# Gather of the sample tile with both parts in one set of rows, and router and low-rank weights as 32 columns

## The reference, cut to what matters

```
# GLA: forget gate through rank 16
gk = log_sigmoid(lr @ w_gk2 + b_gk2) / 16          # lr = x @ w_in[:, 3072:3088]
# MoE: the router picks one group of four experts, then two experts in it
scores = sigmoid(x @ router_w)                     # 16 experts
y = sum_e combine[:, e] * (silu(x @ w_gate[e]) * (x @ w_up[e])) @ w_down[e]
```

## Time and profile before

| | |
|---|---|
| median of 3 runs | 1433.52 us (1432.91 to 1434.7) |
| the profiled execution, its own time | 1435.86 us |
| its span | 1434.1 us |
| PE busy | 1362.3 us, 95%, 7747 instructions |
| PE weight loads | 1138.9 us, 79% |
| DVE busy | 1025.6 us, 72% |
| ACT busy | 763.7 us, 53% |
| POOL busy | 120.1 us, 8% |
| granted TensorE clock, mean | 0.992 |

### The profile page before, as it was taken

One profiled execution on the slowest core, in us unless ns is written; L12 is line 12 of the kernel. 1 busy time (PEld: TensorE's weight loads), 2 busy tenths in 40 slices (PEclk: granted clock), 3 DMA queues, 4 the chain that ended last, 5 costly groups with the idle time before them and its releaser, 6 DMA issues.

```text
span 1434.1 us, 19792 instructions
## 1 busy us (share of the span) xinstructions
PE 1362.3 (95%) x7747; PEld 1138.9 (79%) x7747; DVE 1025.6 (72%) x1097; ACT 763.7 (53%) x788; POOL 120.1 (8%) x194
## 2 busy tenths in 40 slices
PE   6999999999889999999999999999889999999996
PEld 5879898779767788888887799778767788888884
DVE  4444766773547889888898365783548889898986
ACT  4343642432433677676777363332434677676775
POOL 6000045400000000000000014200000000000000
PEclk9999999999999999999999999999999999999998
DMA  8774454425884499899894346435883699898981
GB/s 262 248 233 151 145 177 144 133 91 176 315 331 177 169 335 348 330 337 331 333 343 171 117 151 206 129 118 176 347 323 124 230 336 343 326 348 324 337 335 37
DMA packets 99699, 343.72 MB, mean 240 GB/s; under 512 B 5984, under 2 KB 32112, under 8 KB 70432
## 3 DMA queue, kind: packets, MB, share of 16 engines
q1 hardware_dynamic: 96416, 331.90, 64.5%
q0 software_dynamic: 3200, 10.68, 2.3%
HBM read 327.61 MB, written 14.94 MB: 239 GB/s over the span
## 4 chain that ended last, share of the span: by engine, by line
PE 82%; DVE 11%; ACT 4%; issue 2%; DMA 1%; SPq 0%; DVEq 0%; ACTq 0%
PE ps L1733 64%; PE ps L2211 2%; PE ps L2066 2%; PE ps L2253 1%; PE ps L2088 1%; PE ps L2123 1%; PE ps L1742 1%; DVE mix_s L1460 1%; PE ps L2076 1%; PE ps L2153 1%; DVE x L1198 1%; PE ps L1741 1%; DVE x L1195 1%; PE ps L2202 1%; PE ps L1816 1%
## 5 line engine op out<-in xcount | busy, mean ns | idle before, releaser
L1733 PE MATMUL ps<-w_hi,xt_hi 128*128 128x512 f32 x704 | 280.1, 398 | 14.4 <-DVE w_lo L1131 7.8
L1733 PE MATMUL ps<-w_hi,xt_lo 128*128 128x512 f32 x704 | 276.1, 392 | 0.0
L1131 DVE TENSOR_TENSOR w_lo<-raw,w_hi 128x2048 fp32r<-128x2048 f32 x65 | 148.6, 2294 | 149.1 <-ACT w_hi L740 149.1
L1733 PE MATMUL ps<-w_lo,xt_hi 128*128 128x512 f32 x640 | 251.1, 392 | 0.0
L740 ACT ACTIVATE w_hi<-raw 128x2048 fp32r<-128x2048 f32 x65 | 123.8, 1913 | 163.7 <-PE ps L1733 92.8
L1135 DVE TENSOR_TENSOR moe_lo<-moe_in_raw,w_hi 128x2048 fp32r<-128x2048 f32 x72 | 164.3, 2291 | 29.5 <-ACT w_hi L747 29.3
L1135 DVE TENSOR_TENSOR w_lo<-raw,w_hi 128x2048 fp32r<-128x2048 f32 x72 | 164.9, 2292 | 25.3 <-ACT w_hi L747 24.0
L1733 PEld LDWEIGHTS ps<-w_hi,xt_hi 128*128 128x128 f32 x704 | 133.3, 189 | 45.6 <-issue 10.6
L747 ACT ACTIVATE w_hi<-moe_in_raw 128x2048 fp32r<-128x2048 f32 x72 | 138.1, 1918 | 51.0 <-PE ps L1733 51.0
L1733 PEld LDWEIGHTS ps<-w_hi,xt_lo 128*128 128x128 f32 x704 | 133.2, 189 | 28.6
L747 ACT ACTIVATE w_hi<-raw 128x2048 fp32r<-128x2048 f32 x72 | 137.5, 1912 | 12.0 <-PE ps L1733 12.0
(11 more groups left out here) (380 smaller groups left out, 2375.6 us busy)
## 6 DMA issues: line engine op xcount, KB each, us to landing
raw<-in_moe_w_gate SPq DMA_DIRECT2D x48, 1024.0 KB, 4.9
moe_in_raw<-in_moe_w_down SPq DMA_DIRECT2D x48, 1024.0 KB, 4.9
moe_in_raw<-in_moe_w_up SPq DMA_DIRECT2D x32, 1024.0 KB, 4.9
raw<-in_moe_w_up SPq DMA_DIRECT2D x32, 1024.0 KB, 4.9
raw<-in_xattn_w_kv SPq DMA_DIRECT2D x16, 1024.0 KB, 5.3
raw<-in_hgrn_w_in SPq DMA_DIRECT2D x16, 1024.0 KB, 5.7
raw<-in_cache_mem_k SPq DMA_DIRECT2D x16, 1024.0 KB, 4.9
moe_in_raw<-in_moe_w_gate SPq DMA_DIRECT2D x16, 1024.0 KB, 4.9
```

The costliest lines, as they stand in the source:

```text
L1131: nc.vector.tensor_tensor(lo_at(slot_of(k)), raw_at(slot_of(k)), hi_at(hi_slot(k)).bitcast(F32), ALU.subtract).then_inc(w_low, 1)
L1733: ins = mm(out, lhs, rhs, start=start and n == 0, stop=stop and n == 2, skip_group_check=shared)
```

## The change

1. **Gather.** The sample tile's low part no longer goes to `xn_lo` but to the rows 64 to 127 of `xn_hi`'s third tile, which were zeros. DVE copies the slot numbers of its 64 tokens to these rows too, so one product with `pick` adds both parts. Each gather has five products in place of six. `comb4` gets zeros in these rows, so that "cw" doesn't count a token twice.
2. **Router and low-rank weights.** High and low parts stand side by side as 32 columns, and `both` issues two products for each k-tile in place of three: 32 columns with the high activations, 16 columns (the high ones) with the low activations. The result has 32 rows whose halves have to be added. For the gate this is done by holding `w_gk` twice, in 32 rows (one more small DMA); for the router by multiplying with `pair_sum`, two unit matrices on top of each other, in fp32, where there was a transpose.

```diff
-        w_gk = sb("w_gk", [16, 512])
-        lr_hi = sb("lr_hi", [P, KT, 16], F32R)
-        ...
+        w_gk = sb("w_gk", [32, 512])
+        pair_sum = sb("pair_sum", [2 * EXPERTS, EXPERTS])
+        lr_both = sb("lr_both", [P, KT, 32], F32R)
+        r_both = sb("r_both", [P, KT, 2 * EXPERTS], F32R)
+        lr_hi, lr_lo = lr_both[:, :, 0:16], lr_both[:, :, 16:32]
+        r_hi, r_lo = r_both[:, :, 0:EXPERTS], r_both[:, :, EXPERTS:2 * EXPERTS]
# POOL, at the start
-                     (w_gk[:, :], a["gla_w_gk2"][0]),
+                     (w_gk[0:16, :], a["gla_w_gk2"][0]),
+                     (w_gk[16:32, :], a["gla_w_gk2"][0]),
+            link(nc.gpsimd.memset(pair_sum[:], 0.0))
+            select(pair_sum[:], 1.0, 0, [[-1, EXPERTS]], 1, ALU.not_equal)
+            select(pair_sum[:], 1.0, -EXPERTS, [[-1, EXPERTS]], 1, ALU.not_equal)
# ACT
-                    nc.scalar.activation(st_moe["xn_hi"][:, t, :], x[:, t, :], ...
+                    nc.scalar.activation(st_moe["xn_hi"][0:live(t), t, :], x[0:live(t), t, :], ...
-                nc.scalar.activation(m["rt"][:], ps[0:EXPERTS, 4, 0:TILES * P], ACT.Copy).then_inc(rt_c, 1)
+                nc.scalar.activation(m["rt"][:], ps[0:2 * EXPERTS, 4, 0:TILES * P], ACT.Copy).then_inc(rt_c, 1)
# DVE
-                    nc.vector.tensor_tensor(m["xn_lo"][:, t, :], x[:, t, :], m["xn_hi"][:, t, :].bitcast(F32), ...
+                    low = m["xn_lo"][:, t, :] if t < 2 else m["xn_hi"][64:P, t, :]
+                    nc.vector.tensor_tensor(low, x[0:live(t), t, :], m["xn_hi"][0:live(t), t, :].bitcast(F32), ...
+                link(V_.tensor_copy(u_slot[64:P, 2:3], u_slot[0:64, 2:3]))
-                ins.then_inc(rt_comb, 1)
+                link(ins)
+                V_.memset(comb4[64:P, 2, :], 0.0).then_inc(rt_comb, 1)
# PE
+            def both(out, w, n, hi_x, lo_x, kt):
+                for m_, (rows, v) in enumerate(((2 * n, hi_x), (n, lo_x)) if kt < KT - 1 else ((n, lo_x), (2 * n, hi_x))):
+                    ins = mm(out[0:rows], w[:, 0:rows], v, start=kt == 0 and m_ == 0, stop=kt == KT - 1 and m_ == 1, skip_group_check=True)
+                return ins
# keep_busy
-                pe.wait_ge(rt_w, 1)
-                rows = r_hi[:].rearrange("p k e -> p (k e)")
+                pe.wait_ge(rt_w, 2)
+                rows = r_both[:, 0:4, :].rearrange("p k e -> p (k e)")
# low rank, router
-                        ins = three(ps[0:16, 7, 0:NT], lr_hi[:, kt, :], lr_lo[:, kt, :], xt_hi[:, kt, 0:NT], xt_lo[:, kt, 0:NT], kt == 0, kt == KT - 1, True)
+                        ins = both(ps[0:32, 7, 0:NT], lr_both[:, kt, :], 16, xt_hi[:, kt, 0:NT], xt_lo[:, kt, 0:NT], kt)
-                    ins = three(ps[0:EXPERTS, 4, 0:TILES * P], r_hi[:, kt, :], r_lo[:, kt, :], ...
+                    ins = both(ps[0:2 * EXPERTS, 4, 0:TILES * P], r_both[:, kt, :], EXPERTS, xt_hi[:, kt, :], xt_lo[:, kt, :], kt)
-                    ins = nc.tensor.transpose(ps[:, 5, t * EXPERTS:(t + 1) * EXPERTS], m["rt"][:, t * P:(t + 1) * P], ident[0:EXPERTS, 0:EXPERTS])
+                    ins = mm(ps[:, 5, t * EXPERTS:(t + 1) * EXPERTS], m["rt"][:, t * P:(t + 1) * P], pair_sum[:], start=True, stop=True)
# gather
-                            for r, xx in enumerate((m["xn_hi"], m["xn_lo"])):
+                            for r, xx in enumerate((m["xn_hi"], m["xn_lo"])[0:2 - t // 2]):
```

More of the change, by code:

```diff
@@ L248, in decoder_step @@
         b_gk = sb("b_gk", [P, 4])
-        w_gk = sb("w_gk", [16, 512])
-        lr_hi = sb("lr_hi", [P, KT, 16], F32R)
-        lr_lo = sb("lr_lo", [P, KT, 16], F32R)
-        r_hi = sb("r_hi", [P, KT, EXPERTS], F32R)
-        r_lo = sb("r_lo", [P, KT, EXPERTS], F32R)
+        w_gk = sb("w_gk", [32, 512])
[4 more added lines that the diff above has]
+        r_hi, r_lo = r_both[:, :, 0:EXPERTS], r_both[:, :, EXPERTS:2 * EXPERTS]
         r_bias = sb("r_bias", [P, EXPERTS])
@@ L295, in decoder_step @@
             if l == 1:
-                m["lr_t"] = m["rn"][0:16, :]
+                m["lr_t"] = m["rn"][0:32, :]
             m["states"] = [m["s0"][:, b] for b in range(2 + l)]
@@ L308, in decoder_step @@
             "xn_hi": ([P, TILES, D], F32R), "xn_lo": ([P, TILES, D], F32R), "xg": ([P, D], F32),
-            "rt": ([EXPERTS, TILES * P], F32),
+            "rt": ([2 * EXPERTS, TILES * P], F32),
             "y_hi": ([P, D], F32R), "y_lo": ([P, D], F32R),
@@ L803, in rows_hi @@
                     act.wait_ge(ln_done, TILES * q + t + 1)
-                    nc.scalar.activation(st_moe["xn_hi"][:, t, :], x[:, t, :], ACT.Copy).then_inc(mo[q // 3]["xh"], 1)
+                    nc.scalar.activation(st_moe["xn_hi"][0:live(t), t, :], x[0:live(t), t, :], ACT.Copy).then_inc(mo[q // 3]["xh"], 1)
                 tile_rstd(q, 0)
@@ L883, in _ @@
             transposed(1, TILES)
-            act.wait_ge(consts_in, 160)
-            nc.scalar.activation(lr_hi[:], w_lr[:], ACT.Copy)
-            nc.scalar.activation(r_hi[:], router[:], ACT.Copy).then_inc(rt_w, 1)
+            act.wait_ge(consts_in, 176)
+            nc.scalar.activation(lr_hi, w_lr[:], ACT.Copy)
+            nc.scalar.activation(r_hi, router[:], ACT.Copy).then_inc(rt_w, 1)
             act.wait_ge(consts, 4)
@@ L899, in decay_args @@
                     act.wait_ge(mx_lr, 1)
-                    nc.scalar.activation(m["lr_t"], ps[0:16, 7, 0:NT], ACT.Copy).then_inc(mx_lrc, 1)
+                    nc.scalar.activation(m["lr_t"], ps[0:32, 7, 0:NT], ACT.Copy).then_inc(mx_lrc, 1)
                     for hh in range(4):
@@ L1257, in _ @@
                     dve.wait_ge(consts, 1)
-                    dve.wait_ge(consts_in, 160)
+                    dve.wait_ge(consts_in, 176)
                     nc.vector.tensor_tensor(lb_tmp[:], lb_rows[:, 0, :], lb_rows[:, 1, :], ALU.max).then_inc(consts, 1)
@@ L1273, in _ @@
             dve.wait_ge(rt_w, 1)
-            nc.vector.tensor_tensor(lr_lo[:], w_lr[:], lr_hi[:].bitcast(F32), ALU.subtract)
-            nc.vector.tensor_tensor(r_lo[:], router[:], r_hi[:].bitcast(F32), ALU.subtract).then_inc(rt_w, 1)
+            nc.vector.tensor_tensor(lr_lo, w_lr[:], lr_hi.bitcast(F32), ALU.subtract)
+            nc.vector.tensor_tensor(r_lo, router[:], r_hi.bitcast(F32), ALU.subtract).then_inc(rt_w, 1)
             groups = None
@@ L1575, in _ @@
                     dve.wait_ge(s["xh"], t + 1)
-                    nc.vector.tensor_tensor(m["xn_lo"][:, t, :], x[:, t, :], m["xn_hi"][:, t, :].bitcast(F32), ALU.subtract).then_inc(s["xl"], 1)
+                    low = m["xn_lo"][:, t, :] if t < 2 else m["xn_hi"][64:P, t, :]
+                    nc.vector.tensor_tensor(low, x[0:live(t), t, :], m["xn_hi"][0:live(t), t, :].bitcast(F32), ALU.subtract).then_inc(s["xl"], 1)
                 base = CHUNKS0 if l == 0 else CHUNKS1
@@ L1973, in _ @@
             pe.wait_ge(consts, 1)
-            pe.wait_ge(consts_in, 160)
+            pe.wait_ge(consts_in, 176)
             pe.wait_ge(x_in, 32)
@@ L2167, in _ @@
                 for kt in range(KT):
-                    ins = three(ps[0:EXPERTS, 4, 0:TILES * P], r_hi[:, kt, :], r_lo[:, kt, :], xt_hi[:, kt, :], xt_lo[:, kt, :],
-                                kt == 0, kt == KT - 1, True)
+                    ins = both(ps[0:2 * EXPERTS, 4, 0:TILES * P], r_both[:, kt, :], EXPERTS, xt_hi[:, kt, :], xt_lo[:, kt, :], kt)
                 ins.then_inc(rt_ps, 1)
@@ L2209, in side @@
                         for t in range(TILES):
-                            for r, xx in enumerate((m["xn_hi"], m["xn_lo"])):
+                            for r, xx in enumerate((m["xn_hi"], m["xn_lo"])[0:2 - t // 2]):
                                 ins = mm(ps[:, bank_no, :], m["pick"][:, t, :], xx[:, t, n * NB:(n + 1) * NB],
-                                         start=t == 0 and r == 0, stop=t == TILES - 1 and r == 1)
+                                         start=t == 0 and r == 0, stop=t == TILES - 1)
                     else:
```

## The result

The changed kernel takes 1438.39 us (median of 8 runs, 1437.22 to 1440.42), the kernel before 1434.59 us beside it (8 runs, 1432.91 to 1436.55): a ratio of 1.0028, 95% interval 1.0017 to 1.0039. It is 3.8 us slower where 3.2 us faster were forecast. The profiled execution took 1438.32 us (span 1436.6), 2.46 us more than that of before.

The account below looks back on a forecast made before the run. TensorE was taken to bound the MoE visits. Gather -3.65, low-rank -1.17, pair sum +0.38 and comb links +0.26 gave -4.2 us; +1.0 for the clock made -3.2, so 1430.3 us from 1433.52, range 1428.2 to 1432.8.

Parts of the forecast that it names:

- What bounds the kernel: MoE visits: TensorE's own rate ends them, busy 30.00 of 30.00 us, so each product dropped saves its step.
- Gather in visits, 2.74: Saturated MoE visits: 12 gather products dropped at 0.228 us each save 2.74 us.
- sustained 131 ns: Skill's figure for streamed 512-column products; by it the gathers would give an estimated 2.1 us; the trace's 228 ns was used.
- Gather in front of the first visit, 0.91: Ahead of the first visit, two products dropped per layer: 4 x 0.228 = 0.91 us comes through as well.
- comb links: End of the comb chain: comb4's memset and an extra link add 0.13 us per layer, 0.26 in all.
- u_slot copy: Router stage, in front of the picks: a 0.2 us link, hidden behind 15 fillers, costed at nothing.
- Low-rank, 1.17: Low-rank products at the start of layer 1: 24 become 16, 8 at 0.147 us save 1.17 us.
- Router products at nothing, idle 2.2: Router stage: 1.40 us less TensorE work per layer counts nothing, as ACT's splits delay the copy; TensorE idles 2.2 us.
- Pair sum +0.38: Router stage: fp32 products replacing transposes take 0.56 us against 0.37, +0.19 per layer; ends 0 and +0.4 per layer.
- The clock, +1.0: Router stage: the new idle halves the granted clock with chance 0.6 per layer; about one fall expected, 1.0 us.
- (d): Rival: visits have a second bound just behind TensorE, DMA or DVE, so 2.74 us don't come; 1433.0 us, chance 0.08.
- (e): Rival: slower, as the clock does not recover in the router stage; 1436.7 us or more, chance 0.04.

Follow-up runs that it names:

- eighth run: The whole change, with three small tensors merged so that every other tensor keeps its address of the kernel before; 1433.43 us, 0.9997 of before.
- seventh run: The kernel before with the gather's part of the change alone, nothing allocated, all addresses as before; 1431.33 us, 0.9986 of before.
- twelfth run: The whole change at the addresses of before, plus nine products that compute nothing in TensorE's idle before the wait for copied scores; 1431.69 us, 0.9983 of before.
- first run: The kernel before with an unused 64-byte pad per partition where the change allocates pair_sum, no instruction changed; 1439.85 us, 1.0037 of before.
- ninth run: The router and low-rank part of the change alone, without the gather's edits, other addresses as before; 1436.58 us, 1.0017 of before.

## Why the prediction was wrong

- **What bounds the kernel: right as a place, short as a reading.** The visits are TensorE's. But "a product that is gone is time that is gone" took the step of 0.228 us as fixed for the products that stay. It is no property of the product: in the second block shown it is 5.44 / 24 = 0.227 us before and 0.232 with one allocation moved. This is the step that failed: the sum has no term for moved buffers, and they cost 0.72 us in a full visit, in all 4.4 us by the ratios of the eighth run and 5.3 by the rows below.
- **Gather in visits, 2.74: right.** 75.41 to 74.95 us at the old addresses, 0.46 per visit in six visits, 2.76. The prediction had set this step against the sustained 131 ns that the Trainium skill states (page "TensorE: Matmul & The Clock Gate", section "Back-to-back issue gap"); with 2.76 us the runs agree with 0.228 us and not with that figure.
- **Gather in front of the first visit, 0.91: wrong.** 0.06 per layer arrives (seventh run), comb links included, where 0.46 less 0.13 were counted. The forecast named the picks as what the gather waits for; it waits for `n_last`, the end of the chain in which the u_slot copy is one more link. That copy was costed at nothing. The comb links, costed at 0.26 in all, stand further down on the same path, whose end sets PE's wait for w_lo.
- **Low-rank, 1.17: right.** 3.52 - 2.33 = 1.19.
- **Router products at nothing, idle 2.2: right.** Copy at 4.62, idle 2.17.
- **Pair sum +0.38: undersized.** 0.84 in place of 0.35 us per layer, +0.98 in all. The row taken has 4 columns, these products have 16; an idle ahead of them is not the reason, since in the twelfth run they take 0.84 without one. It is a little beyond the upper end that was kept, 0.4 per layer.
- **The clock, +1.0: mechanism right, number of falls wrong.** A fall in the router stage costs 1.14 to 1.15 us at the gather, near the 1.0 taken for one, and by the path named, the 12 fillers. But another one can come in the first visit (1.57), for which the sum had nothing. The eighth and twelfth run put the mean over executions at about 2 us rather than 1.0, roughly, and at the old addresses. Part 1 of the Trainium skill's page "TensorE: Matmul & The Clock Gate" has the clock gated down when the array is idle. The filled idle agrees; the changed kernel's idle of 2.17 us without a fall shows that the length of the idle alone does not decide.
- **Addresses: absent**, as term and as rival. (d) foresaw a second bound in the visits, but as a wait, and there is none. (e) had the sign, by a clock that stays low; no profile shows that (and its border of 1436.7 is a slip: 1433.5 + 2.9 is 1436.4).

The sum from the runs, for the profiled executions, with no fall in the router stages or visits of either: the twelfth run's stage ends 317.01 us behind the router's first product (461.91), before 317.92 (461.36), after 319.65 (460.42). These are the rows of its last scatter, in the order before, after, twelfth:

```profile
779.28 0.50 PE ps L2202
```
```profile
780.07 0.50 PE ps L2215
```
```profile
778.92 0.50 PE ps L2215
```

The instructions of the change are worth -0.91 us per layer, the addresses +2.64. Two layers and the low-rank products: 2 x (2.64 - 0.91) - 1.19 = +2.3 us. The two profiled executions differ by 2.46, but that they agree so closely is luck in part: the router's first product of layer 0 comes 0.94 us earlier after (460.42 and 461.36), that of layer 1 0.85 us later (1101.47 and 1100.62), and 1.79 - (2.64 - 0.91) + 1.19 = 1.25 us between the two lie in no term. The medians differ by 3.8; of the 1.3 us more, nearly all is that the profiled execution of before (1435.86) lay 1.27 above its median.

**What stays open** is the mechanism behind the addresses. By the Trainium skill, page "SBUF — State Buffer", section "SBUF: two separate sides", engine and DMA sides can't contend with each other, and engines contend only at the port that VectorE and GpSimd share; GpSimd is idle in the visits (0.00 in the row of 690 to 720). By that rule a pad would change nothing, and the first run measured +5.7 us; the measurement decides. The same instructions with other addresses suggest that accesses to the buffers get in each other's way, but no run shows this, nor which engine or DMA would take part: none takes one engine's accesses away.

## What to carry to other kernels

When a saturated stage gets slower with the same instructions and no wait, compare the length of one repeated block, then what the edit did to the allocation order; put a new small tensor where it moves nothing, or test the kernel before with a pad of its size. Work that is removed in front of a wait on another engine is an idle and can cost the clock: move what is waited for forward in the same edit (4.4 us here), or fill the hole (about 2.0). For a step in front of such a wait, name the last link of the chain that releases it: here a new link of 0.15 us, 0.18 to the next one's start, came through with 0.16.

## What the runs showed of the hardware

- A shift of 64 bytes between two groups of buffers changes the time of 24 products of 512 columns from 5.44 to 5.57 us in some blocks, leaves others at 5.57, and costs the kernel 5.7 us by the medians (1.0037). A visit takes 0.71 us more, with 128 bytes 0.52; moving everything together costs nothing (1.0005).
- The loss grows with the groups that are moved: 0.26 us of a visit for the rows, picks and h, 0.54 with moe_hi, 0.71 with all that lies ahead of them in the first run.
- An idle of 2.15 us was followed by half the granted clock in both layers of one execution, one of 2.17 us in the changed kernel by none, and in the ninth run's profile by a fall in one layer of the two (1.14 us at the gather). One fall came behind an idle of 1.32 us (seventh run). Nine empty products in the idle brought back 2.0 us by the ratios, with intervals that overlap a little.
